# Eight matmuls on a constant tile at the start, and one single-use weight buffer instead of two

## The chip, the cores and the metric

The kernel runs on one core of a Trainium2 chip. The metric is the time of one execution in microseconds (us), here the median of several runs. TensorE is called PE in the profile, its weight load PEld, VectorE DVE, ScalarE ACT, GpSimd POOL, and SyncE, which issues most of the transfers, SP.

## The reference, cut to what matters

Two transformer blocks over 256 tokens of width 1024, all in float32. The first has three branches (spatial gating, convolution, pooling), a dense feed-forward and a gated embedding. The second has two kinds of attention and a mixture of 32 experts:

```python
def reference(x, ...):
    x = first_block(x, p, ...)       # rms_norm, w_in, three branches, w_out, feed-forward, embedding
    return second_block(x, c_2, ...) # attention, then experts, then a last rms_norm

def expert_block(args):              # for each of the 32 experts, on the tokens routed to it
    xb, e = args
    return (jax.nn.silu(xb @ w_gate[e]) * (xb @ w_up[e])) @ w_down[e]
```

The first step is `rms_norm(x, g_mix_pre)` and its product with `w_in`. The experts' weights are 3 x 1024 x 512 numbers for each expert, and all 32 are read whoever is routed to them.

## The kernel before, in words

Each engine has its own list of instructions, written by hand, and waits on semaphores. All weights pass once from HBM. There are two streams, both issued by SP in one fixed order.

The first stream, `load` (line 2338), brings the weights of everything but the experts, in pieces of 1 MB, into four buffers `raw`. For each piece ACT writes a rounded copy (`sph`, line 1180), POOL writes the remainder (`spl`, line 2310), and PE uses both in three matmuls (lines 492 to 494).

The second stream (line 2381) brings the experts' weights: `EXPERT_WEIGHTS` lists 192 pieces of 1 MB, four of gate and up weights (`in_gu`) for expert x and then two of down weights (`in_dn`) for expert x-1. Piece s goes into buffer `SLOT[place(s)]`. There are NS = 20 buffers that are used in turn: 18 halves of `ring0` to `ring8`, one at `ar(3072, 2048)`, and `slotx`. Two more are used once, at `ar(6144, 2048)` for piece 3 and `ar(8192, 2048)` for piece 4. Most buffers lie where something of the stages before lay, so each first use has a wait of its own in the loop that ends in line 2381. From piece 22 on, a piece waits until PE has used the piece that held its buffer before:

```python
                elif old:
                    kind0, x0, j0 = EXPERT_WEIGHTS[old[-1]]
                    if kind0 == "gu":
                        w.wait_ge(gu_mm, 4 * x0 + j0 + 1)
                    else:
                        w.wait_ge(down_mm, 2 * x0 + j0 + 1)
                e.dma_start(SLOT[i], I[kind][x, j]).then_inc(slot_sem[i], 16)
```

For each expert PE runs `gate_up` (line 1078), `turn` (lines 1093, 1099), `down` (line 1114) and `scatter` (line 1125), and for every fourth expert `gather` (line 1058). At the end come the last squares, roots and four stores.

The small tiles of the expert stage (`HN`, `SWT`, `HS`, `XG`, `YP`, `GFI`) lie in the same area `ar` as the single-use buffers.

At the start the work goes like this. SP loads `x` in two halves and then the first pieces. ACT squares each half (line 1220), takes the root (line 1194), DVE inverts it (line 1662), ACT makes a diagonal matrix of it (line 1199), and PE multiplies each block of `x` by the diagonal, which scales and transposes it (`norm_tile`, line 485; each such float32 matmul stands in the trace as two). Behind its two diagonals ACT has in its list the rounded copy of the first piece of weights (`split_one`), and only then the rounded copies of the normalized `x` (`high`, line 1208, tile `xah`). DVE writes the remainders (`low`, line 1677, tile `xal`), and PE's first product with weights waits for them. DVE's first instruction is the memset of a one-column tile `blank`, which ACT reads to load a table (`warm`, line 1170).

Of the kernel before, what the change touches and what calls it, by code (L numbers as in the profile page):

```python
# [20 lines left out]
NRAW = 4  # L21
# [79 lines left out]
def k8(t):  # L101
    return t.rearrange("p (k n) -> p k n", k=8)
# [105 lines left out]
def program(nc, I, out, const_at):  # L208
    with ExitStack() as ctx:
# [3 lines left out]
        ps = [ctx.enter_context(nc.psum_tensor(f"ps{i}", [128, 512], F32)) for i in range(8)]  # L213
        base = (nc.sbuf_base + 31) // 32 * 32

        def at(name, off, n, dt=F32, parts=128):

            assert base + 4 * (off + n) <= nc.sbuf_usable_end, (name, off, n)
            return nc.alloc_sbuf_tensor_at(name, [parts, n], dt, offset=base + 4 * off)[:, :]
# [29 lines left out]
        def ar(off, n, k=None):  # L249
            ar_n[0] += 1  # L250
            v = at(f"ar{ar_n[0]}", O_AR + off, n)
            return v if k is None else v.rearrange("p (k n) -> p k n", k=k)

        units, first, ada_at, ff_at, wide_at, conv_at = stream_plan()
# [2 lines left out]
        G = ar(0, 6144, 24)  # L257
        CV = ar(6144, 8 * 286, 8)
        CVO = ar(8432, 2048, 8)
        U = ar(10480, 2048, 8)  # L260
        V = ar(12528, 2048, 2)
        ZP = ar(12528, 8 * 272, 8)
# [40 lines left out]
        CWS = at("cws", O_XA + 1312, 36)  # L303

        SQA, SQ2 = ar(2048, 256), [ar(2304 + 256 * n, 256) for n in range(2)]
        HN = ar(1024, 2048, 2)
        w_out_units = [units[first["w_out_2"] + n] for n in range(4)]
        RING = ([at(f"ring{n}", TOP - 4096 - 4096 * n, 4096) for n in range(2)] +
                [at("ring2", O_RAW, 4096), at("ring3", O_XB, 4096), at("ring4", O_RAW + 4096, 4096)])
# [4 lines left out]
        SLOT = [r[:, 2048 * i:2048 * i + 2048] for r in RING for i in range(2)]  # L314
        SLOT.insert(8, ar(3072, 2048))
        SLOT.append(at("slotx", O_X, 2048))
        NS = len(SLOT)

        ONCE = {3: NS, 4: NS + 1}
        SLOT += [ar(6144, 2048), ar(8192, 2048)]  # L320

        def place(s):

            return ONCE.get(s, (s - (2 if s > 4 else 0)) % NS)

        RT = at("RT", 3040, 72).rearrange("p (t n) -> p t n", t=2)
        WC = at("WC", 3112, 64).rearrange("p (t n) -> p t n", t=2)
# [2 lines left out]
        FLAG = at("FLAG", 3368, 1, I32)  # L330
        SW = [ar(256 * n, 256) for n in range(2)]
        SE = [ar(512 + 256 * n, 256) for n in range(2)]
        SWT = [ar(6144 + 256 * n, 256) for n in range(2)]
        HS = [ar(6656 + 256 * n, 256) for n in range(2)]
        HE = [ar(10240 + 128 * n, 128) for n in range(2)]
        YP = [ar(8192 + 1024 * n, 1024) for n in range(2)]
        o_xg = (const_at["dist"][0] + 7) // 8 * 8
        XG = [k8(at("xg0", o_xg, 1024)), k8(ar(7168, 1024))]
        GFI = at("gfi", o_xg, 1024)
        JUNK, OUT = RING[4][:, 0:512], RING[5][:, 0:2048].rearrange("p (t n) -> p t n", t=2)  # L340


# [9 lines left out]
        def tap(k, c):  # L352
# [26 lines left out]
        slot_sem = [sem(f"d_slot{i}") for i in range(NS - NRAW)] + raw_sem  # L379
        d_x0, d_x1, d_idn, d_cst, d_col = (sem(n) for n in ("d_x0", "d_x1", "d_idn", "d_cst", "d_col"))  # L380
        d_ws, d_gmp, d_ada, d_gfp, d_p, d_wr, d_gfi, d_out = (sem(n) for n in (
            "d_ws", "d_gmp", "d_ada", "d_gfp", "d_p", "d_wr", "d_gfi", "d_out"))
        slot_sem += [d_gfp, d_wr]

        hi_ok, lo_ok, half_used = sem("hi_ok"), sem("lo_ok"), sem("half_used")

# [61 lines left out]

            return QK[kind][64 * (h % 2):64 * (h % 2) + 64, h // 2, :]

        slot_landed, per_slot = {}, [0] * (NS - NRAW) + [16 * sum(u.slot == i for u in units) for i in range(NRAW)] + [16, 16]
        for s, entry in enumerate(EXPERT_WEIGHTS):
            per_slot[place(s)] += 16
            slot_landed[entry] = per_slot[place(s)]
# [5 lines left out]
        def tensor(e):  # L460
            w = Seq(e)
# [112 lines left out]
            def channel_mean(name, src):  # L574

                b = bank(name)
                claim(b)
                e.matmul(ps[b][:, 0:256], mean, src, start=True, stop=True).then_inc(w.up(mean_mm), 1)
                return b


            cb = bank("conv")
# [67 lines left out]
            u = units[first["pool"]]  # L650
# [511 lines left out]
        def scalar(e):  # L1162
            w = Seq(e)
            begun = [0]

            def warm(func):

                w.wait_ge(blank_ok, 1)
                w.wait_ge(warm_ok, w.n(warm_ok))
                e.activation(warmed, blank, func).then_inc(w.up(warm_ok), 1)  # L1170

# [115 lines left out]
            for n in range(12):  # L1287
# [4 lines left out]
                if n == 8:  # L1292
                    w.wait_ge(cc_ok, 1)
                    w.wait_ge(mix_ok, 12)
                    e.activation(SQ, CVO, ACTF.Square).then_inc(w.up(sq_ok), 1)
            w.wait_ge(mean_mm, 2)
# [4 lines left out]
            def silu(c0):  # L1301

                w.wait_ge(cn_ok, 2)
                for c in (c0, c0 + 1):
                    e.activation(CVO[:, c, :], CVO[:, c, :], ACTF.Silu, bias=col("b_conv_ln", c),
                                 scale=col("g_conv_ln", c)).then_inc(w.up(silu_ok), 1)
# [16 lines left out]
            for n in range(4):  # L1323
                e.activation(XB[0][:, 2 * n:2 * n + 2, :], CVO[:, 2 * n:2 * n + 2, :], ACTF.Copy)\
                    .then_inc(w.up(act_hi), 1)
# [324 lines left out]
        def vector(e):  # L1650
            w = Seq(e)
# [45 lines left out]
            def conv(n, pairs=4):  # L1697

                for _ in range(n):
# [5 lines left out]
                    if k:  # L1705
                        w.wait_ge(tap_ok, w.n(tap_ok) - 1)
                        e.scalar_tensor_tensor(out=acc if k < 30 else CVO[:, c, :], in0=CV[:, c, k:k + 256],  # L1707
                                               scalar=tap(k, c), in1=acc, op0=ALU.mult, op1=ALU.add)\
# [5 lines left out]
                    tapped[:] = (pair, k, 1) if not i else (pair, k + 1, 0) if k < 30 else (pair + 1, 0, 0)  # L1714


            e.memset(blank, 1.0).then_inc(w.up(blank_ok), 1)
            w.wait_ge(d_idn, 16)
            for tt in range(2):
# [39 lines left out]
            def mix(i):  # L1759
# [10 lines left out]
                own()  # L1770
                e.tensor_tensor(k2(ps[b]), k2(ps[b]), U[:, 2 * i:2 * i + 2, :], ALU.mult).then_inc(w.up(mix_ok), 1)

# [13 lines left out]
            own()  # L1786
            e.tensor_reduce(TMP[:, 0:256], CVO.rearrange("p k n -> p n k"), AX, ALU.add).then_inc(w.up(cs_ok), 1)
            w.wait_ge(z_ok, 4)
# [530 lines left out]
        def sync(e):  # L2319
            w = Seq(e)  # L2320

            def load(a, b):

                for v in range(a, b):
                    u = units[v]
                    if v == first["qs1"]:
                        w.wait_ge(half_used, 2 * units[wide_at[10]].n + 2)
                        for i in range(2):
                            e.dma_start(SLOT[i], I["gu"][0, i]).then_inc(slot_sem[i], 16)
                    if v >= NRAW:  # L2330
                        old = units[v - NRAW]
                        if old.half:
                            w.wait_ge(lo_ok, 2 * old.n + 2)
                        elif v - NRAW in ada_at:
                            w.wait_ge(ada_ok, ada_used[ada_at.index(v - NRAW)])
                        else:
                            w.wait_ge(pool_mm, 4)
                    e.dma_start(RAW[u.slot], I["stream"][v]).then_inc(raw_sem[u.slot], 16)

            e.dma_start(X[:, 0, :], I["x"][0, 0:128, :]).then_inc(d_x0, 16)  # L2340
            e.dma_start(X[:, 1, :], I["x"][0, 128:256, :]).then_inc(d_x1, 16)
            load(0, NRAW)
            e.dma_start(CST[:, e0:cst_w], I["cst"][:, e0:cst_w]).then_inc(d_cst, 16)
            load(NRAW, len(units))

            def raws_free(*raws):

                for v in range(len(units) - NRAW, len(units)):
                    if units[v].slot in raws:
                        w.wait_ge(lo_ok, 2 * units[v].n + 2)  # L2350

            for s, (kind, x, j) in enumerate(EXPERT_WEIGHTS):
                i = place(s)
                old = [t for t in range(s) if place(t) == i]
                if s < 2:
                    continue
                if s == 2:
                    w.wait_ge(dt_mm, 8)
                elif s == 3:
                    w.wait_ge(dv_mm, 2)  # L2360
                elif s == 6:
                    raws_free(0, 1)
                elif s == 8:
                    w.wait_ge(half_used, 2 * units[first["vs"] + 1].n + 2)
                elif s == 10:
                    w.wait_ge(sv_mm, 2)
                elif s == 11:
                    raws_free(2)
                elif s == 12:
                    raws_free(3)  # L2370
                elif 13 <= s < 21:
                    w.wait_ge(half_used, 2 * w_out_units[min((s - 11) // 2, 3)].n + 2)
                elif s == 21:
                    w.wait_ge(y0_mm, 1)
                elif old:
                    kind0, x0, j0 = EXPERT_WEIGHTS[old[-1]]
# [6 lines that stand above are left out]
            for tt in range(2):  # L2383
                for nn in range(2):
                    c = slice(nn * 512, nn * 512 + 512)
                    w.wait_ge(*((fin_ok, 7 + tt) if nn else (so_ok, 7 + 3 * tt)))
                    e.dma_start(out[0, 128 * tt:128 * tt + 128, c], OUT[:, tt, c]).then_inc(d_out, 16)
# [177 lines left out]
```

## Time and profile before

| | |
|---|---|
| time, median of 3 runs | 1126.35 us (1125.43 to 1130.05) |
| the profiled execution, its own time | 1130.05 us |
| its span, first to last instruction | 1128.2 us |
| PE busy | 1029.6 us, 91% of the span |
| DVE, ACT, POOL busy | 507.7, 377.3, 494.0 us |
| moved by DMA | 342.16 MB, mean 303 GB/s |

All times of rows are counted from the span's start. The profiled execution is the slowest of the three. The 1.85 us between its time and its span lie outside of the instructions. A row of busy tenths has 40 slices of 28.2 us each.

### The profile page before, as it was taken

The numbers are of one execution on the slowest core, as the hardware profiler recorded it, in microseconds if no ns is written. First come the engines' busy times: TensorE is split into PE (matmuls) and PEld (weight loads), VectorE is DVE, ScalarE is ACT, GpSimd is POOL, SyncE is SP. The second block draws the span as 40 slices with busy tenths as digits, with TensorE's granted clock in tenths as the row PEclk, the third lists the DMA queues.
The fourth block names the chain that finished last, engine by engine and source line by source line (L and its number), as shares of the span: only waits on it lengthen the run. The fifth ranks groups of instructions, "written<-read, shape, count | busy, mean of one in ns | idle before, by whom it ended". The sixth has DMA issues, their size and how long they took to land.

```text
span 1128.2 us, 19730 instructions
## 1 busy us (share of the span) xinstructions
PE 1029.6 (91%) x8494; PEld 791.5 (70%) x8494; DVE 507.7 (45%) x904; ACT 377.3 (33%) x537; POOL 494.0 (44%) x209
## 2 busy tenths in 40 slices
PE   7999999999999999998999999899988778878677
PEld 6989999999799998887998895343443333424232
DVE  2998977565357666214345643322221221212113
ACT  7355544643663434446595332000000000000002
POOL 6886899867687777988565410000000000000000
PEclk9999999999999999999999999999999998989998
DMA  9554455456579888757333879999999999999995
GB/s 364 202 187 174 161 183 174 170 201 243 181 253 356 311 341 326 298 186 266 127 138 145 330 321 405 421 419 420 420 420 421 420 420 420 421 421 419 422 419 205
DMA packets 48330, 342.16 MB, mean 303 GB/s; under 512 B 5361, under 2 KB 5745, under 8 KB 7410
## 3 DMA queue, kind: packets, MB, share of 16 engines
q1 hardware_dynamic: 46944, 337.56, 75.6%
q10 hardware_dynamic: 1298, 3.32, 0.8%
q8 instruction: 68, 1.11, 0.4%
q14 instruction: 20, 0.16, 0.0%
HBM read 339.81 MB, written 1.05 MB: 302 GB/s over the span
## 4 chain that ended last, share of the span: by engine, by line
PE 60%; DMA 27%; DVE 5%; POOL 3%; ACT 3%; SPq 1%; issue 1%; DVEq 0%; ACTq 0%
DMA ring<-in_gu 19%; PE ps L492 14%; PE ps L494 14%; PE ps L493 14%; PE ps L1078 5%; DMA raw<-in_stream 4%; PE ps L1125 4%; POOL spl L2310 3%; DMA slotx<-in_dn 2%; PE ps L1114 2%; PE ps L1058 2%; SPq L2381 1%; PE ps L485 1%; ACT sph L1180 1%; DVE ps L1868 1%
## 5 line engine op out<-in xcount | busy, mean ns | idle before, releaser
L2310 POOL TENSOR_TENSOR spl<-raw,sph 128x1024 fp32r<-128x1024 f32 x204 | 493.6, 2451 | 162.3 <-ACT sph L1180 162.2
L1180 ACT ACTIVATE sph<-raw 128x1024 fp32r<-128x1024 f32 x204 | 205.8, 1053 | 144.6 <-DMA raw<-in_stream 91.9
L492 PE MATMUL ps<-xbh,sph 128*128 128x256 f32 x608 | 173.0, 285 | 5.8 <-DVE ps L1941 1.8
L493 PE MATMUL ps<-xbl,sph 128*128 128x256 f32 x608 | 172.0, 283 | 0.0
L494 PE MATMUL ps<-xbh,spl 128*128 128x256 f32 x608 | 172.0, 283 | 0.0
L492 PE MATMUL ps<-xah,sph 128*128 128x256 f32 x576 | 165.0, 286 | 1.1 <-DVE xal L1677 0.8
L493 PE MATMUL ps<-xal,sph 128*128 128x256 f32 x576 | 163.0, 283 | 0.0
L494 PE MATMUL ps<-xah,spl 128*128 128x256 f32 x576 | 162.9, 283 | 0.0
L2244 DVE TENSOR_TENSOR ar<-ar,ps 64x256 f32<-64x256 f32 x32 | 13.5, 423 | 266.5 <-ACT ar L1615 266.5
L1615 ACT ACTIVATE ar<-ps 64x256 f32<-64x256 f32 x32 | 12.1, 378 | 339.7 <-PE ps L1078 339.7
L1125 PE MATMUL ps<-ar,ar 128*128 128x512 f32 x256 | 123.9, 628 | 0.0
L492 PEld LDWEIGHTS ps<-xbh,sph 128*128 128x128 f32 x608 | 116.6, 192 | 7.4 <-DVE ps L1941 3.4
L494 PEld LDWEIGHTS ps<-xbh,spl 128*128 128x128 f32 x608 | 116.7, 192 | 0.0
L493 PEld LDWEIGHTS ps<-xbl,sph 128*128 128x128 f32 x608 | 116.6, 192 | 0.0
L492 PEld LDWEIGHTS ps<-xah,sph 128*128 128x128 f32 x576 | 110.5, 192 | 2.3 <-DVE xal L1677 0.9
L493 PEld LDWEIGHTS ps<-xal,sph 128*128 128x128 f32 x576 | 110.5, 192 | 0.4 <-issue 0.2
L494 PEld LDWEIGHTS ps<-xah,spl 128*128 128x128 f32 x576 | 110.5, 192 | 0.0
L1125 PEld LDWEIGHTS ps<-ar,ar 128*128 128x128 f32 x256 | 48.3, 199 | 64.7 <-issue 64.7
L1707 DVE SCALAR_TENSOR_TENSOR ps<-ar,COL,ps 128x256 f32<-128x256 f32 x232 | 92.1, 483 | 0.0
L1114 PE MATMUL ps<-ring,ar 128*32 128x512 f32 x456 | 56.9, 600 | 22.9 <-DVE ar L2252 13.8
L1078 PE MATMUL ps<-ring,ar 128*32 128x256 f32 x912 | 60.3, 395 | 17.9 <-DMA ring<-in_gu 17.8
L1078 PE MATMUL ps<-ring,xg 128*32 128x256 f32 x912 | 59.1, 397 | 11.7 <-DMA ring<-in_gu 11.7
(297 smaller groups left out, 1333.7 us busy)
## 6 DMA issues: line engine op xcount, KB each, us to landing
raw<-in_stream SPq DMA_DIRECT2D x127, 1024.0 KB, 5.1
ring<-in_gu SPq DMA_DIRECT2D x114, 1024.0 KB, 26.8
ring<-in_dn SPq DMA_DIRECT2D x57, 1024.0 KB, 27.1
ar<-in_gu SPq DMA_DIRECT2D x8, 1024.0 KB, 18.8
slotx<-in_gu SPq DMA_DIRECT2D x6, 1024.0 KB, 27.4
ar<-in_dn SPq DMA_DIRECT2D x4, 1024.0 KB, 27.7
slotx<-in_dn SPq DMA_DIRECT2D x3, 1024.0 KB, 26.3
X<-in_x SPq DMA_DIRECT2D x2, 512.0 KB, 4.7
```

Source lines behind the costliest of these rows:

```text
L492: e.matmul(o, sh, mh, start=start, stop=False)
L493: e.matmul(o, sh, ml, start=False, stop=False)
L494: return e.matmul(o, sl, mh, start=False, stop=stop)
L1058: mm = e.matmul(ps[b][:, (k - k0) * 128:(k - k0) * 128 + 128], HN[:, tt, k * 128:k * 128 + 128], SE[n][:, tt * 128:tt * 128 + 128], start= ...
L1078: mm = e.matmul(ps[b][32 * q:32 * q + 32, 0:256], XG[g % 2][:, k, (x % 4) * 32:(x % 4) * 32 + 32], W[:, q // 2, k % 2, (q % 2) * 256:(q % ...
L1114: mm = e.matmul(ps[bb[nn]][32 * j:32 * j + 32, :], HE[x % 2][:, 32 * j:32 * j + 32], W[:, 2 * (j % 2) + j // 2, :], start=True, stop=True)
L1125: mm = e.matmul(ps[yb[tt * 2 + nn]][:, :], SWT[x % 2][:, tt * 128:tt * 128 + 128], YP[x % 2][:, nn * 512:nn * 512 + 512], start=False, sto ...
L1180: e.activation(u.half(SPH[u.n % NSP], h), u.half(RAW[u.slot], h), ACTF.Copy).then_inc(w.up(hi_ok), 1)
L1615: e.activation(HS[x % 2][0:64, :], ps[bank_of["gu", x]][0:64, 0:256], ACTF.Silu)\
L1707: e.scalar_tensor_tensor(out=acc if k < 30 else CVO[:, c, :], in0=CV[:, c, k:k + 256], scalar=tap(k, c), in1=acc, op0=ALU.mult, op1=ALU.add)\
L2244: e.tensor_tensor(h[0:64, :], h[0:64, :], ps[bank_of["gu", x]][64:128, 0:256], ALU.mult)\
L2310: e.tensor_tensor(u.half(SPLO[u.n % NSP], h), u.half(RAW[u.slot], h), u.half(SPH[u.n % NSP], h), ALU.subtract).then_inc(w.up(lo_ok), 1)
```

## The change

It has two parts.

1. A tile `FILL` of 384 columns is set to 1.0 by DVE ahead of the memset of `blank`. PE waits for both memsets and then runs eight float32 matmuls of 128x128 by 128x256 on it, into bank 7, ahead of its first `norm_tile`. Nothing reads their result. ACT's `warm` waits for both memsets too.

2. Of the two single-use buffers the one at `ar(6144, 2048)` is gone. Piece 3 goes into buffer 3 of the ring, piece 4 into the single-use buffer at `ar(8192, 2048)`, and each later piece into the buffer after the one it had. The waits in SP's list are written for the piece numbers that now stand at the same buffers; piece 3 has no wait of its own, and piece 4 waits for the first `dv_mm` where piece 3 had waited for the second. `HN` moves to the area set free; `SWT`, `HS` and one `XG` move to where `HN` was, and the other `XG` to where the first `XG` was. `GFI` moves with its `XG`.

```diff
--- before.py
+++ after.py
@@ -257,6 +257,7 @@
         G = ar(0, 6144, 24)
         CV = ar(6144, 8 * 286, 8)
         CVO = ar(8432, 2048, 8)
+        FILL = ar(10480, 384)
         U = ar(10480, 2048, 8)
         V = ar(12528, 2048, 2)
         ZP = ar(12528, 8 * 272, 8)
@@ -303,7 +304,7 @@
         CWS = at("cws", O_XA + 1312, 36)
 
         SQA, SQ2 = ar(2048, 256), [ar(2304 + 256 * n, 256) for n in range(2)]
-        HN = ar(1024, 2048, 2)
+        HN = ar(6144, 2048, 2)
         w_out_units = [units[first["w_out_2"] + n] for n in range(4)]
         RING = ([at(f"ring{n}", TOP - 4096 - 4096 * n, 4096) for n in range(2)] +
                 [at("ring2", O_RAW, 4096), at("ring3", O_XB, 4096), at("ring4", O_RAW + 4096, 4096)])
@@ -316,12 +317,12 @@
         SLOT.append(at("slotx", O_X, 2048))
         NS = len(SLOT)
 
-        ONCE = {3: NS, 4: NS + 1}
-        SLOT += [ar(6144, 2048), ar(8192, 2048)]
+        ONCE = 4
+        SLOT.append(ar(8192, 2048))
 
         def place(s):
 
-            return ONCE.get(s, (s - (2 if s > 4 else 0)) % NS)
+            return NS if s == ONCE else (s - (s > ONCE)) % NS
 
         RT = at("RT", 3040, 72).rearrange("p (t n) -> p t n", t=2)
         WC = at("WC", 3112, 64).rearrange("p (t n) -> p t n", t=2)
@@ -330,13 +331,12 @@
         FLAG = at("FLAG", 3368, 1, I32)
         SW = [ar(256 * n, 256) for n in range(2)]
         SE = [ar(512 + 256 * n, 256) for n in range(2)]
-        SWT = [ar(6144 + 256 * n, 256) for n in range(2)]
-        HS = [ar(6656 + 256 * n, 256) for n in range(2)]
+        SWT = [ar(1024 + 256 * n, 256) for n in range(2)]
+        HS = [ar(1536 + 256 * n, 256) for n in range(2)]
         HE = [ar(10240 + 128 * n, 128) for n in range(2)]
         YP = [ar(8192 + 1024 * n, 1024) for n in range(2)]
-        o_xg = (const_at["dist"][0] + 7) // 8 * 8
-        XG = [k8(at("xg0", o_xg, 1024)), k8(ar(7168, 1024))]
-        GFI = at("gfi", o_xg, 1024)
+        XG = [k8(ar(2048, 1024)), k8(at("xg1", (const_at["dist"][0] + 7) // 8 * 8, 1024))]
+        GFI = ar(2048, 1024)
         JUNK, OUT = RING[4][:, 0:512], RING[5][:, 0:2048].rearrange("p (t n) -> p t n", t=2)
 
 
@@ -380,7 +380,7 @@
         d_x0, d_x1, d_idn, d_cst, d_col = (sem(n) for n in ("d_x0", "d_x1", "d_idn", "d_cst", "d_col"))
         d_ws, d_gmp, d_ada, d_gfp, d_p, d_wr, d_gfi, d_out = (sem(n) for n in (
             "d_ws", "d_gmp", "d_ada", "d_gfp", "d_p", "d_wr", "d_gfi", "d_out"))
-        slot_sem += [d_gfp, d_wr]
+        slot_sem.append(d_wr)
 
         hi_ok, lo_ok, half_used = sem("hi_ok"), sem("lo_ok"), sem("half_used")
 
@@ -448,7 +448,7 @@
 
             return QK[kind][64 * (h % 2):64 * (h % 2) + 64, h // 2, :]
 
-        slot_landed, per_slot = {}, [0] * (NS - NRAW) + [16 * sum(u.slot == i for u in units) for i in range(NRAW)] + [16, 16]
+        slot_landed, per_slot = {}, [0] * (NS - NRAW) + [16 * sum(u.slot == i for u in units) for i in range(NRAW)] + [16]
         for s, entry in enumerate(EXPERT_WEIGHTS):
             per_slot[place(s)] += 16
             slot_landed[entry] = per_slot[place(s)]
@@ -577,6 +577,11 @@
                 claim(b)
                 e.matmul(ps[b][:, 0:256], mean, src, start=True, stop=True).then_inc(w.up(mean_mm), 1)
                 return b
+
+
+            w.wait_ge(blank_ok, 2)
+            for _ in range(8):
+                e.matmul(ps[7][:, 0:256], FILL[:, 0:128], FILL[:, 128:384], start=True, stop=True)
 
 
             cb = bank("conv")
@@ -1165,7 +1170,7 @@
 
             def warm(func):
 
-                w.wait_ge(blank_ok, 1)
+                w.wait_ge(blank_ok, 2)
                 w.wait_ge(warm_ok, w.n(warm_ok))
                 e.activation(warmed, blank, func).then_inc(w.up(warm_ok), 1)
 
@@ -1714,6 +1719,7 @@
                     tapped[:] = (pair, k, 1) if not i else (pair, k + 1, 0) if k < 30 else (pair + 1, 0, 0)
 
 
+            e.memset(FILL, 1.0).then_inc(w.up(blank_ok), 1)
             e.memset(blank, 1.0).then_inc(w.up(blank_ok), 1)
             w.wait_ge(d_idn, 16)
             for tt in range(2):
@@ -2356,21 +2362,21 @@
                     continue
                 if s == 2:
                     w.wait_ge(dt_mm, 8)
-                elif s == 3:
-                    w.wait_ge(dv_mm, 2)
-                elif s == 6:
+                elif s == ONCE:
+                    w.wait_ge(dv_mm, 1)
+                elif s == 5:
                     raws_free(0, 1)
-                elif s == 8:
+                elif s == 7:
                     w.wait_ge(half_used, 2 * units[first["vs"] + 1].n + 2)
+                elif s == 9:
+                    w.wait_ge(sv_mm, 2)
                 elif s == 10:
-                    w.wait_ge(sv_mm, 2)
+                    raws_free(2)
                 elif s == 11:
-                    raws_free(2)
-                elif s == 12:
                     raws_free(3)
-                elif 13 <= s < 21:
-                    w.wait_ge(half_used, 2 * w_out_units[min((s - 11) // 2, 3)].n + 2)
-                elif s == 21:
+                elif 12 <= s < 20:
+                    w.wait_ge(half_used, 2 * w_out_units[min((s - 10) // 2, 3)].n + 2)
+                elif s == 20:
                     w.wait_ge(y0_mm, 1)
                 elif old:
                     kind0, x0, j0 = EXPERT_WEIGHTS[old[-1]]
```

## Rows read from the trace of the kernel before

**Rows 1.** The page: slices of the span, and the chain that ended last by line.
```profile
PE   7999999999999999998999999899988778878677
PEclk9999999999999999999999999999999998989998
DMA  9554455456579888757333879999999999999995
DMA ring<-in_gu 19%; PE ps L492 14%; PE ps L494 14%; PE ps L493 14%; PE ps L1078 5%; DMA raw<-in_stream 4%; PE ps L1125 4%; POOL spl L2310 3%; DMA slotx<-in_dn 2%; PE ps L1114 2%; PE ps L1058 2%; SPq L2381 1%; PE ps L485 1%; ACT sph L1180 1%; DVE ps L1868 1%
```

**Rows 2.** The chain that ended last, its start: start, duration, what.
```profile
0.75 4.04 DMA X<-in_x
7.10 4.36 PE ps L485 x20
11.55 1.57 ACT xah L1208 x4
```

**Rows 3.** The timeline of the start: start, duration, instruction, idle before and releaser.
```profile
0.82 0.06 DVE L1717 MEMSET SM<- 128x1 f32 x1 [0.82 <-PEq L2553]
1.66 1.28 ACT L1170 ACT_TABLE_LOAD   x1 [1.66 <-PEq L2553]
8.85 0.40 ACT L1199 ACTIVATE ar<-cst,SM 128x128 f32<-128x128 f32 x1 [0.23 <-DVE SM L1662]
9.15 1.99 ACT L1180 ACTIVATE sph<-raw 128x1024 fp32r<-128x1024 f32 x2
11.55 1.57 ACT L1208 ACTIVATE xah<-ps,COL 128x256 fp32r<-128x256 f32 x4 [0.41 <-PE ps L485]
12.42 4.33 DVE L1677 SCALAR_TENSOR_TENSOR xal<-ps,COL,xah 128x256 fp32r<-128x256 f32 x8 [3.61 <-ACT xah L1208]
```

**Rows 4.** Two windows of norm_tile: busy us and count of each engine, PEclk, DMA share, GB/s.
```profile
7.10:10.90 3.80, 3.80 (x18) 3.80 (x19) 0.17 (x1) 3.50 (x6) 0.63 (x1) 1.00 0.99 414
11.07:12.79 1.72, 1.72 (x16) 1.53 (x14) 0.37 (x1) 1.31 (x5) 1.72 (x2) 1.00 1.00 419
```

**Rows 5.** Other float32 rows: L659 in the chain, and the one wide memset of DVE.
```profile
227.09 6.91 PE ps L659 x32
L1884 DVE MEMSET ar<- 128x1024 f32 x1 | 0.9, 912 | 0.3 <-DVE pt L1687 0.3
```

**Rows 6.** What PE waited for between 16.5 and 300 us: total, times, longest.
```profile
PE ps L492 <- POOL spl L2310: 1.8, 3, 0.7
```

**Rows 7.** SP's issues of pieces 2 to 5, 12 to 13, 21, and 22 to 24.
```profile
617.57 0.33 SPq L2381 DMA_DIRECT2D ring<-in_gu  x1
622.97 1.52 SPq L2381 DMA_DIRECT2D ar<-in_gu  x2
624.53 0.43 SPq L2381 DMA_DIRECT2D ring<-in_gu  x1
...
656.57 0.81 SPq L2381 DMA_DIRECT2D ring<-in_gu  x2
...
675.96 0.33 SPq L2381 DMA_DIRECT2D slotx<-in_dn  x1
...
682.90 2.27 SPq L2381 DMA_DIRECT2D ring<-in_gu  x3
```

**Rows 8.** Windows of the expert stage, columns as in Rows 4.
```profile
683.00:685.00 2.00, 2.00 (x44) 1.17 (x37) 0.00 (x0) 0.38 (x2) 0.00 (x0) 1.00 0.59 160
695.00:1105.00 410.00, 342.48 (x3329) 156.13 (x3327) 93.21 (x204) 21.51 (x57) 0.00 (x0) 0.96 1.01 420
1100.00:1105.00 5.00, 4.61 (x22) 1.87 (x22) 0.00 (x0) 0.00 (x0) 0.00 (x0) 0.67 1.02 424
```

**Rows 9.** The chain that ended last: first DMA wait of the expert stage, and its end.
```profile
811.03 26.34 DMA slotx<-in_dn
...
1074.01 26.34 DMA ring<-in_gu
...
1100.39 1.94 PE ps L1078 x16
1102.33 4.12 PE ps L1125 x8
1106.45 1.91 PE ps L1078 x32
...
1112.43 3.63 PE ps L1125 x8
1116.06 1.85 PE ps L1114 x16
1117.91 0.05 issue
1117.96 1.11 PE ps L1125 x2
```

## The prediction, made before the changed kernel was run

> **What bounds the kernel now.** I read the slices of the page first [rows 1]. PE is busy nearly everywhere up to the 24th slice, and from the 25th on the DMA digit is 9 and PE's share falls. So there are two stages with different limits: up to about 680 us the time is made by PE and what feeds it, behind that by the experts' weights coming in. The chain by line says the same: the three matmul lines of the dense part hold 14% each, and `ring<-in_gu` alone 19% [rows 1]. Since the change touches the first 12 us and the buffers of the experts' stream, I then read those two places closely.
>
> At the start the chain goes x landing at 4.79, ACT, then PE's `norm_tile` from 7.10 for 20 rows and 4.36 us, then ACT's `xah` at 11.55 [rows 2]. The timeline adds what the chain hides: between its second diagonal (8.85) and `xah` ACT rounds the first weights, from 9.15 to 11.14, and only 0.41 us of idle stands between that and `xah` [rows 3]. Behind it DVE writes eight `xal` without a gap, 12.42 to 16.75, and PE's first product waits for them.
>
> The clock: the granted column reads 1.00 in both windows of `norm_tile`, but nothing is recorded that early, and the spacing of the rows tells more. 18 rows in 3.80 us are 211 ns each, 16 rows in 1.72 us are 108 ns each [rows 4]. The same instruction doubles its rate near 11.0 us, so it ran at 1.2 GHz before and at 2.4 GHz behind. PE had done nothing before 7.10; the clock rose 3.9 us after it began.
>
> In the expert stage the window 695 to 1105 has a DMA share of 1.01 and 420 GB/s [rows 8]. Nothing that PE does there can bring the weights faster. The last wait of the chain is a piece issued at 1074.01 that takes 26.34 us; from its landing at 1100.35 PE works to 1119.07 with hardly a wait [rows 9].
>
> **Part one, the filler.** DVE's only other wide memset takes 912 ns for 1024 columns [rows 5]; 384 columns are about 0.35 us. DVE starts at 0.82, so `blank` is ready near 1.3 instead of 0.9, and ACT's table load stands at 1.66 [rows 3]: hidden. If it were not, the next cover is the landing of x, two us behind the end of the table load.
>
> PE then starts near 1.4. Eight float32 matmuls are 16 rows of 256 columns. L659 has this shape and runs 32 rows in 6.91 us, 216 ns each at full clock [rows 5]; at half clock twice the 211 ns of 128 columns, 0.42 us. If the clock rises 3.9 us after the start, as it did behind 7.10, then nine rows run to 5.3 and seven take 1.5 us: the filler ends at 6.8, before `norm_tile` can begin. At half clock throughout it ends at 1.4 + 16 x 0.42 = 8.1.
>
> At full clock the first tile's 16 rows take 1.72 us from 7.10, the second waits for its diagonal at 9.25, and the 20th row, which releases `xah`, ends near 9.9 instead of 11.46. With the filler ending at 8.1 it is 8.1 + 20 x 0.108 + 0.2 = 10.5. Either way ACT is in `split_one` until 11.14 and is late next. So of 1.85 us that PE gains (18 rows x 0.103) only ACT's idle 0.41 us reaches `xah`. DVE's eight `xal` start from that, and PE's products from them. I take -0.4 us. The bounds are -1.9, if all of it counted, and +1.2, if the clock stayed low over filler and tiles (20 rows from 8.1 at 211 ns end at 12.6 against 11.46).
>
> The Trainium skill, "TensorE: Matmul & The Clock Gate", section "HAM oscillation — how this bites in real kernels", prices low clock at the throttled time times one half. By it 3.9 us are worth 2.0 us, and the sum below would end at +0.5 instead of +2.1. That rule prices PE's own time; it has no engine beside PE that is late anyway, as ACT is here.
>
> Does the 0.4 us reach the experts? PE's waits from 16.5 to 300 us come to 1.8 us in all [rows 6], and the rest of the way to 682 is chained by waits on one another, and between the first slice and the 25th the DMA digit is 9 once only [rows 1]. Nothing there is tied to a fixed time, so I let it pass whole.
>
> **Part two, the buffers.** No instruction is added on any engine; tiles only change their place, so `HN`, `SWT`, `HS`, `XG` and `GFI` cost nothing in themselves (a bank effect, if any, has no row; I take 0). What changes is how many pieces can be on chip before PE frees one. I counted the issues in SP's list. Before, four pieces (2 to 5) go out between 617.57 and 624.53 [rows 7]; then SP waits for the raw buffers. After, three pieces (2 to 4) fill the buffers that are free, and SP reaches the same wait with piece 5. From there each wait stands at the same buffer, so the same event sends a piece numbered one less: at 656.57 pieces 11 and 12 instead of 12 and 13, at 675.96 piece 20 instead of 21. When the first `gate_up` frees buffer 0 at 682.90, piece 21 goes out instead of 22. Piece 24 can go out a little earlier than 25 did, since buffer 3 now holds piece 3 and is free after PE's fourth step. From piece 25 on the predecessor is the piece 20 before, as it was.
>
> SP's own order: piece 3 no longer waits for `dv_mm`, and behind it only piece 4 was queued, which also goes earlier. That helps nothing, because all of it lands long before 682.
>
> So at 682.9 one piece more is still to come, and from then on DMA has no gap but 0.8 us just there: in 683 to 685 its share is 0.59 [rows 8], the same in both kernels. A piece is 1024 KB; at 420 GB/s that is 2.50 us. PE asks for pieces faster than they come, so the piece that ends the chain lands 2.50 us later. Bounds: 0 if the missing piece were made up in some gap (none is left after 685), and 3.3 if the gap of 0.8 came on top. I take +2.5, the value that the rows of the stage itself give.
>
> **Sum.** -0.4 + 2.5 = +2.1 us, with ends at -1.9 and +4.5. The profiled execution, 1130.05 us with a span of 1128.2, would be 1132.15 with a span of 1130.3. It lies 3.7 us above the median of the runs shown, so on the median, 1126.35, I forecast 1128.4 us, slower by 0.2%. A measurement of this kernel tells about 0.5% (5.6 us) from no change, so this is no change.
>
> **Rivals.** (a) The missing piece costs nothing: its place would be a gap in the stream after 685. For it: the chain meets no wait on DMA in this stage before 811 [rows 9]. Against it: the share of 1.01 over 410 us. Time: 1126.35 - 0.4 = 1125.9. (b) The clock's gain passes whole, -1.9, if ACT's wait on PE counted more than the profile shows; 1126.35 - 1.9 + 2.5 = 1126.9. Against it stands ACT busy until 11.14. (c) The filler does not raise the clock or comes too late: +1.2 + 2.5, 1130.1. For it: I know only one rise, and it came after 3.9 us. (d) Slower beyond 0.5%: the tail runs at half clock. From 1100.39 to 1119.07 PE's rows on the chain are 1.94, 4.12, 1.91, 3.63, 1.85, 1.11 and smaller ones, some 17 us [rows 9], and PE comes to them from waiting for weights. In 1100 to 1105 the granted clock was 0.67 [rows 8], so about 3.3 us were at 1.2 GHz, and a scatter took 4.12 instead of 3.63. A stretch of low clock costs half its length; with +2.1 given, 3.5 us more are needed, that is 7 us more at half clock. With an earlier starved PE this could happen in many executions: 1132 or more.
>
> On (d) the Trainium skill, the same page, section "Loop structure matters more than you think", says that a long wait for a transfer between matmuls drops the clock and the next ones run at half rate. It speaks against this change; the trace agrees in kind (0.96 over the stage [rows 8]) and not in size.
>
> **How the numbers follow.** My forecast 0.60, (a) 0.16, (b) 0.10, (c) 0.07, (d) 0.04, and 0.03 for something faster beyond 0.5% that no row shows. The forecast's own range is 1127 to 1130. Taking in the bounds of the sum (1124.5 to 1130.9) and that executions of one kernel lie up to 3.7 us above their median, the range is 1124.6 to 1131.4. Within 0.5%: 0.60 + 0.16 + 0.10 + 0.07 = 0.93; slower 0.04; faster 0.03.
>
> **What the profile of the changed kernel would show.** 16 rows of the filler from about 1.4 us; `norm_tile` at 108 ns a row; `xah` at about 11.15 with no idle on PE's account; PE's first product 0.4 us earlier; the first issue behind the raw wait unchanged but for that shift, `slotx` again near 675.5, buffer 0 near 682.5; DMA share 1.01 to the end, and a last gate piece that lands at 1102.4 instead of 1100.35. Wrong would be: `xah` well before 11.1 (then something else stood in ACT's list), a last landing at or before 1100.3, or a tail of more than 19 us from that landing to the end of PE's rows.

## The result, and the profile after

The changed kernel takes 1133.17 us (median of 4 runs, 1132.1 to 1134.09) beside 1126.36 us (4 runs, 1125.43 to 1130.05). The ratio is 1.0051 with a 95% interval of 1.003 to 1.0074, that is 5.7 us more (3.4 to 8.3). I had forecast 1128.4 and a range up to 1131.4. The record has nine more executions of the changed kernel; the median of all thirteen is 1132.15 us (1129.79 to 1137.22), 1.0 less than that of the four.

The profiled execution of after took 1130.97 us, 0.92 more than that of before, where I had forecast 2.1 more. It is a fast one of its kernel (the third of thirteen), while that of before is the slowest of its four, so their difference can't be read as that of the kernels. What each stage took can be compared. First the head of the page of after:

```profile
span 1128.9 us, 19763 instructions
PE   8999999999999999998999998989978888888676
PEclk9999999999999999999999999999998999989899
DMA  9555455456479898756344689999999999999994
PE 57%; DMA 27%; POOL 5%; DVE 4%; ACT 3%; SPq 2%; issue 1%; DVEq 0%; ACTq 0%
```

The shape is that of [rows 1]: PE nearly everywhere until the 24th slice, DMA at 9 behind it. Now the start, from the timeline of after (start, length, what, idle before and its releaser):

```profile
0.90 0.38 DVE L1722 MEMSET ar<- 128x384 f32 x1 [0.90 <-PEq L2559]
1.35 5.50 PE L584 MATMUL ps<-ar 128*128 128x256 f32 x16 [1.35 <-DVE SM L1723]
1.66 1.28 ACT L1175 ACT_TABLE_LOAD   x1 [1.66 <-PEq L2559]
5.05 1.06 ACT L1225 ACTIVATE ar<-X 128x1024 f32<-128x1024 f32 x1 [1.90 <-DMA X<-in_x]
7.34 4.25 PE L485 MATMUL ps<-ar,X 128*128 128x128 f32 x32 [0.48 <-ACT ar L1204]
9.39 1.99 ACT L1185 ACTIVATE sph<-raw 128x1024 fp32r<-128x1024 f32 x2
11.28 0.45 ACT L1213 ACTIVATE xah<-ps,COL 128x256 fp32r<-128x256 f32 x1
12.14 4.33 DVE L1682 SCALAR_TENSOR_TENSOR xal<-ps,COL,xah 128x256 fp32r<-128x256 f32 x8 [3.09 <-ACT xah L1213]
```

The filler runs from 1.35 to 6.85 and the table load stays at 1.66, as forecast. Behind the filler `norm_tile` needs 1.86 us for its first 16 rows, 116 ns each where the first rows took 211 in [rows 4], so it runs at 2.4 GHz from its start. `xah` no longer waits for PE (no idle in its row, 0.41 us in [rows 3]): it follows `sph`. x landed 0.23 us later here, so the starts don't show the gain. The time from ACT's first square of x to `xah` does: 6.73 us before (4.82 to 11.55), 6.23 here.

The windows of after (length, busy time and rows of PE, PEld, DVE, ACT and POOL, granted clock, DMA share, GB/s), which answer to [rows 8]:

```profile
683.00:685.00 2.00, 2.00 (x46) 1.14 (x38) 0.13 (x1) 0.38 (x1) 0.00 (x0) 1.00 1.00 373
695.00:1105.00 410.00, 342.78 (x3310) 154.20 (x3309) 91.00 (x198) 19.99 (x53) 0.00 (x0) 0.95 1.01 420
1100.00:1105.00 5.00, 5.00 (x42) 2.12 (x40) 0.00 (x0) 0.00 (x0) 0.00 (x0) 1.00 1.01 419
```

The weights come at the same 420 GB/s. The first line doesn't answer to that of [rows 8], since the stage began 4.5 us earlier here; at the same place in the stage, 678.5 to 680.5, the DMA share is 0.60 (0.59 before), so the short gap is there in both. SP's list, from the timeline of after, shows the pieces that [rows 7] showed before:

```profile
613.09 0.80 SPq L2387 DMA_DIRECT2D ring<-in_gu  x2
615.88 0.33 SPq L2387 DMA_DIRECT2D ar<-in_gu  x1
630.66 2.02 SPq L2387 DMA_DIRECT2D ring<-in_gu  x3
671.46 0.33 SPq L2387 DMA_DIRECT2D slotx<-in_dn  x1
678.41 0.33 SPq L2387 DMA_DIRECT2D ring<-in_dn  x1
```

Three pieces (2 to 4) go out, and then SP waits. The first piece that waits for `gate_up` is now a down piece, number 21, where it was a gate piece, number 22. So one piece more is still to come.

The end of the chain, which answers to [rows 9]:

```profile
1080.51 27.74 DMA ar<-in_dn
1108.25 0.04 issue
1108.30 1.06 PE ps L1119 x8
...
1110.20 3.63 PE ps L1130 x8
1113.83 1.85 PE ps L1119 x16
1115.69 0.05 issue
1115.73 1.11 PE ps L1130 x2
```

All of PE's rows here are at full clock. The chain now hangs on piece 189, a down piece. The forecast had named the gate piece 185, which the chain hung on before, and 1102.4 for its landing; it landed at 1098.35, which by the forecast's own list is a sign of being wrong. It is none, since the stage began 4.5 us earlier: counted from the first expert matmul it landed 2.49 us later than before, as forecast. From 1108.25 to the end of PE's rows it is 8.6 us. What I had not read lies behind the last store. SP's waits in 1123 to 1130, first before, then after (in all, times, longest):

```profile
SPq L2389 <- PEq L2389: 0.2, 1, 0.2
SPq L2398 <- PEq L2398: 0.2, 1, 0.2
```

```profile
SPq L2404 <- PEq L2404: 3.2, 1, 3.2
SPq L2395 <- PEq L2395: 0.2, 1, 0.2
```

SP's last wait on PE has grown from 0.2 to 3.2 us. Between the two waits stands a branch: `with nc.If(flag > 0)` in `general`, which jumps over the code for a case that doesn't occur with this input. Every engine takes it. Its instructions, in the listing of that line (min/median/max ns, first and last start), before and after:

```profile
L2399 ACTq COMPARE_BRANCH  x1: 50/50/50, 1127.0 to 1127.0; - x1
L2399 PEldq COMPARE_BRANCH  x1: 369/369/369, 1127.1 to 1127.1; - x1
L2399 SPq COMPARE_BRANCH  x1: 50/50/50, 1127.6 to 1127.6; - x1
```

```profile
L2405 ACTq COMPARE_BRANCH  x1: 50/50/50, 1124.8 to 1124.8; - x1
L2405 PEldq COMPARE_BRANCH  x1: 3729/3729/3729, 1124.9 to 1124.9; - x1
L2405 SPq COMPARE_BRANCH  x1: 50/50/50, 1125.4 to 1125.4; - x1
```

The same branch takes 0.37 us on PE before and 3.73 us after, and the same 0.05 to 0.07 us as before on the other engines. From the first store's issue to the span's end it is 4.85 us before (1123.35 to 1128.2) and 7.82 after (1121.12 to 1128.94), 2.97 us more. That is a little less than the 3.36 us on PE: before, PE was through at 1127.45 and SP came to its own branch only at 1127.6, so part of PE's time lay behind SP's.

The spans come out of their stages as follows; the last landing is that of piece 191.

| us | before | after |
|---|---|---|
| to the first expert matmul | 681.77 | 677.28 |
| from there to the last landing | 433.41 | 435.90 |
| from there to the first store's issue | 8.17 | 7.95 |
| from there to the end | 4.85 | 7.82 |
| span | 1128.20 | 1128.94 |

The second line is the buffer, +2.49. The fourth is the branch, +2.97. The first hides most of both in this pair: 4.5 us less, of which the filler can have given 0.5 and the rest is a spread between executions (last section).

### The profile page after: what moved, and what is told of

Same layout as the page of the kernel before. It is cut to its first block, busy times and chain, and to the rows that moved or that the text cites. A ratio compares the mean times of both kernels' runs of the same rounds, so it can differ in the third digit from the quotient of the medians.

```text
span 1128.9 us, 19763 instructions
## 1 busy us (share of the span) xinstructions
PE 1033.6 (92%) x8510; PEld 792.3 (70%) x8510; DVE 508.8 (45%) x905; ACT 376.9 (33%) x537; POOL 494.0 (44%) x209
## 4 chain that ended last, share of the span: by engine, by line
PE 57%; DMA 27%; POOL 5%; DVE 4%; ACT 3%; SPq 2%; issue 1%; DVEq 0%; ACTq 0%
DMA ring<-in_gu 15%; PE ps L492 13%; PE ps L494 13%; PE ps L493 13%; PE ps L1083 5%; POOL spl L2316 5%; DMA raw<-in_stream 5%; PE ps L1130 4%; DMA ar<-in_gu 3%; DMA ar<-in_dn 2%; DMA ring<-in_dn 2%; PE ps L1119 2%; PE ps L1063 2%; SPq L2387 2%; ACT sph L1185 1%
## 5 line engine op out<-in xcount | busy, mean ns | idle before, releaser
L1083 PE MATMUL ps<-ring,xg 128*32 128x256 f32 x928 | 62.4, 402 | 18.0 <-DMA ring<-in_gu 17.8
L1083 PEld LDWEIGHTS ps<-ring,xg 128*32 128x32 f32 x928 | 28.3, 113 | 58.6 <-issue 31.4
```

The lines of the kernel that those rows point to most:

```text
L1083: mm = e.matmul(ps[b][32 * q:32 * q + 32, 0:256], XG[g % 2][:, k, (x % 4) * 32:(x % 4) * 32 + 32], W[:, q // 2, k % 2, (q % 2) * 256:(q % ...
```

## The experiments

In all of them the branch's duration on PE and the stage times are read from one profile each, the medians from several runs. The median of before was 1126.47 us beside the first four kernels (32 runs), 1127.5 beside the next four (18 runs) and 1126.98 beside the last three (21 runs).

My theory: three terms add up, the filler's -0.4, the buffer's +2.5, and +3.0 from PE's branch, whose place in the program the filler's 32 PE instructions (16 matmul rows and 16 weight loads) have moved. (The expectations below count the whole 3.4 us of PE's branch; 3.0 of them reach the end.) The rivals: the filler costs time in some other way (its work, its tile, the clock); the longer branch comes from the smaller number of buffers; the buffer's price is not a piece.

**One part each.** The first kernel is before with the filler alone, the second before with one single-use buffer alone.

```diff
+            w.wait_ge(blank_ok, 2)
+            for _ in range(8):
+                e.matmul(ps[7][:, 0:256], FILL[:, 0:128], FILL[:, 128:384], start=True, stop=True)
... (cut: the tile FILL and the second memset that `warm` waits for, as in the change)
+            e.memset(FILL, 1.0).then_inc(w.up(blank_ok), 1)
```

> Part one alone: the kernel before with the filler of eight matmuls, both single-use buffers kept. Theory J (the filler's 32 PE instructions move the branch behind the expert stage, so that its target has to be fetched): PE's branch at the very end lasts about 3.7 us instead of 0.37, and the kernel is 3.4 - 0.4 = 3.0 us slower than before. Rival W (the forecast's own working: the filler only helps): branch 0.4 us, kernel 0.4 us faster. Rival B (all of the loss comes with the buffer): no slower than before.

Measured: 1131.05 us (1128.37 to 1133.59, 9 runs), ratio 1.0038 (1.0023 to 1.0053), that is +4.3 us (2.6 to 6.0). The branch took 3869 ns.

```diff
-        ONCE = {3: NS, 4: NS + 1}
-        SLOT += [ar(6144, 2048), ar(8192, 2048)]
+        ONCE = 4
+        SLOT.append(ar(8192, 2048))
... (cut: the waits and the moved tiles, as in the change)
```

> Part two alone: one single-use buffer, no filler. The forecast's term: 2.5 us slower than before, branch at the end 0.37 us as before, DMA share 1.01 from 695 on, and at the time when the first buffer of the ring is freed the piece issued is number 21. Rival B: 6 to 7 us slower, all that was measured. Rival J2 (the buffer costs nothing, everything is the branch): within 0.5 us of before.

Measured: 1130.01 us (1126.6 to 1133.58, 12 runs), ratio 1.0029 (1.0015 to 1.0043), +3.3 us (1.7 to 4.8). The branch took 475 ns, and from the first expert matmul to the last landing it was 435.96 us. So the branch belongs to the filler, and the piece to the buffer.

**The branch's place without the filler's work.** Before, with 64 waits on a semaphore that has long been reached, at the start of PE's list. They compile to 32 instructions, as many as the filler has.

```diff
+            for _ in range(64):
+                e.wait_ge(blank_ok, 1)
             cb = bank("conv")
```

> The kernel before with 64 waits on a semaphore that is already up ahead of PE's first matmul, which compile to 32 instructions: as many as the filler has, no work for TensorE and no warmer clock; PE is idle there until 7.1 us and 32 of them need some 2 us. Theory J: branch at the end 3.7 us, kernel 3.4 us slower than before. Rival (the filler's matmuls themselves cost the time, by clock or by contention): no change, branch 0.37 us.

Measured: 1129.82 us (1126.96 to 1133.08, 12 runs), ratio 1.0015 (0.9996 to 1.0034), +1.7 us (-0.5 to 3.8). The interval holds 0, 3.0 and the 3.4 of the expectation, so the times decide nothing; the profile does. The listing of the branch's line:

```profile
L2401 ACTq COMPARE_BRANCH  x1: 50/50/50, 1124.8 to 1124.8; - x1
L2401 PEldq COMPARE_BRANCH  x1: 3839/3839/3839, 1124.8 to 1124.8; - x1
```

With no filler and with both buffers the branch is long. So what the instructions ahead of it do is not what counts.

**The filler with half the instructions.** After, with four matmuls of 512 columns instead of eight of 256: the same columns, 16 instructions.

```diff
-        FILL = ar(10480, 384)
+        FILL = ar(10480, 640)
...
-            for _ in range(8):
-                e.matmul(ps[7][:, 0:256], FILL[:, 0:128], FILL[:, 128:384], start=True, stop=True)
+            for _ in range(4):
+                e.matmul(ps[7][:, 0:512], FILL[:, 0:128], FILL[:, 128:640], start=True, stop=True)
```

> The changed kernel with the filler as four matmuls of 512 columns: the same work for PE in 16 instructions instead of 32. Theory J: the branch stands 16 instructions earlier; if its target is then in what PE has fetched, the branch lasts 0.37 us and the kernel is 2.5 - 0.4 = 2.1 us slower than before, as forecast; if not, 3.7 us and 5.5 us slower. Rival (the loss grows with the filler's work, not with its instructions): as the changed kernel, 6.8 us slower, with a short branch.

Measured: 1129.72 us (1128.18 to 1132.0, 12 runs), ratio 1.0029 (1.0016 to 1.0041), +3.3 us (1.8 to 4.6):

```profile
L2405 PEldq COMPARE_BRANCH  x1: 475/475/475, 1125.0 to 1125.0; - x1
```

The branch is short again, and from the first expert matmul to the last landing it is 436.5 us, 3.1 more than before. Beside the kernel with one buffer and no filler (+3.3 us, on the same chip) this one shows the filler with a short branch: the two measured the same, so no cost or gain of it shows there.

**The version that the terms point to.** Both single-use buffers and the filler of four matmuls.

> The kernel before with both single-use buffers and the filler as four matmuls of 512 columns (16 PE instructions, few enough to keep the branch short). Forecast of both causes together (branch 3.4, buffer 2.5, filler -0.4): branch 0.4 to 0.5 us, from PE's first expert matmul to the last landing 433.4 us as before, and 0.4 us faster than before, which is within the scatter of the runs. If the filler costs something by itself that the branch does not explain: 1 to 2 us slower.

Measured: 1128.57 us (1125.42 to 1132.98, 12 runs) beside 1127.5, ratio 1.0012 (0.9997 to 1.0027). The branch took 378 ns, and the stage to the last landing 433.7 us. The expected -0.4 us lies just outside of the interval (-0.3 to 3.0 us). The same kernel once more, on another chip:

> Filler as four matmuls of 512 columns, both single-use buffers, once more, since its first interval (-0.3 to +3.0 us) left open whether the filler helps or costs. Filler's gain: 0.4 us faster than before. Filler costs something: 1 us slower or more.

1128.01 us (1126.09 to 1134.71, 11 runs) beside 1126.98, ratio 1.0012 (0.9995 to 1.0028). Neither measurement shows a gain.

**More places of the branch.** Before with 256 and with 128 instructions more, as 16 or 8 waits ahead of each `gate_up`, one execution each.

```diff
                 if x < NE:
+                    for _ in range(16):
+                        e.wait_ge(blank_ok, 1)
+                if x < NE:
                     gate_up(x, (0, 1))
```

> The kernel before with 16 more waits on a semaphore that is up ahead of each expert's first gate_up, which compile to 8 PE instructions each, 256 in all: one whole block of PE's program as its fetches are seen in the trace (16 KB each, 64 bytes an instruction). If what counts is where the branch stands within a block: 0.4 us, like before. If more PE instructions in general lengthen it: 3.7 us or more.

> The same with 8 waits ahead of each expert, 128 instructions in all: half a block. If the place within a block counts, the target is in a block not yet fetched: 3.7 us, although there are fewer instructions than in the kernel with 256. If only the number counts, it would lie with the longer one.

Measured, the branch's line with 256 more (one execution of 1125.26 us) and with 128 more (1129.67 us):

```profile
L2402 PEldq COMPARE_BRANCH  x1: 375/375/375, 1122.3 to 1122.3; - x1
```

```profile
L2402 PEldq COMPARE_BRANCH  x1: 3772/3772/3772, 1123.7 to 1123.7; - x1
```

256 instructions more leave the branch short, 128 make it long. It is not their number in itself but where the branch comes to lie in a pattern that 256 instructions leave as it was.

**No single-use buffer.** Before with 20 buffers only, no filler.

> Part two doubled: no single-use buffer at all, no filler. The buffer's theory: another 2.5 us, 5.0 us slower than before; from PE's first expert matmul to the last landing 433.4 + 5.0 = 438.4 us; branch 0.4 us. Rival (only the first lost buffer counts, since the gap in the stream moves): 2.5 us, 435.9 us.

Measured: 1131.88 us (1129.87 to 1138.03, 7 runs), ratio 1.0047 (1.0028 to 1.0066), +5.3 us (3.2 to 7.4). First expert matmul to last landing: 438.2 us. Two buffers 433.4, one 435.9, none 438.2: a piece each.

**Sixteen instructions, no filler.** The 64 waits cut to 32.

> Control for it: the kernel before with 32 waits at PE's start, 16 instructions, no filler. Branch 0.4 us; the same as before. Against the kernel with the filler it shows the filler alone at the same place of the branch: 0.4 us slower than that one by the forecast.

Measured: 1127.43 us (1125.83 to 1133.08, 11 runs), ratio 1.0007 (0.9992 to 1.0023). The branch took 475 ns.

**After with a short branch.** After with 14 waits ahead of each `gate_up`, 224 instructions, so that the filler's 32 and they are 256.

> The changed kernel whole (eight filler matmuls, one single-use buffer) with 7 more PE instructions ahead of each expert, 224 in all, so that with the filler's 32 the branch stands one whole block (256) later than in the kernel before. If the place of the branch is what the forecast missed: branch 0.4 to 0.5 us instead of 3.7, and 2.1 us slower than before, as forecast for the change, instead of the 5.7 to 6.8 that the change showed. If the filler or the moved tiles cost something else: slower by 5 us or more with a short branch.

Measured: 1130.52 us (1129.9 to 1132.67, 5 runs), ratio 1.0043 (1.0028 to 1.0058), +4.9 us (3.2 to 6.5):

```profile
L2408 PEldq COMPARE_BRANCH  x1: 369/369/369, 1126.8 to 1126.8; - x1
```

The branch is short once more, though the filler is all there. But the expected 2.1 us are missed: the time is 2.8 us above the -0.4 + 2.5 of the other two terms, and the interval shuts them out. Of this, 0.8 us shows in the profile: 436.7 us to the last landing instead of 435.9. The added waits stand in that stage, but the 4x512 kernel took 436.5 there without them. The rest is open. Against after itself, which was measured apart from it, this kernel is 2.7 us faster by the median of the four executions and 1.6 by that of the thirteen, where the branch should give 3.0.

All kernels by the branch:

| instructions more on PE | kernels | branch on PE, ns | first store's issue to the end, us |
|---|---|---|---|
| 0 | before, one buffer, no buffer | 369 to 475 | 4.8 to 4.9 |
| 16 | 4x512 filler (two kernels, one of them twice), 32 waits | 378 to 475 | 4.8 to 4.9 |
| 32 | after, filler alone, 64 waits | 3729 to 3869 | 7.8 to 8.0 |
| 128 | waits | 3772 | 7.9 |
| 256 | waits, after with waits | 375, 369 | 4.8 to 4.9 |

## Why the forecast missed

**The step that failed** is the costing of part one by what its instructions do at the start. The prediction counts 16 rows of the filler in PE time and opens part two with "No instruction is added on any engine"; nowhere does it ask what 32 more PE instructions do to the rest of the program. They move the branch at the end. The missing term is +3.0 us. It read the end only up to the PE row that ends at 1119.07; the 4.85 us between the first store's issue and the end, where the branch of before stands with its 0.37 us, were taken as fixed without being read.

What the branch waits for is shown in part. The DMA view of after has one more transfer of instructions in the window 1124 to 1130 than that of before, here before and then after (packets, MB, share):

```profile
q8 instruction: 1, 0.02, 1.3%
```

```profile
q8 instruction: 2, 0.03, 2.5%
```

The added one starts at 1125.9, 1.0 us after PE's branch began, and carries 16 KB; the other one starts in both kernels 0.7 us after the branch has ended. Ahead of the branch this queue had made 67 transfers for 17201 recorded instructions of PE, which is 64 bytes for each and 256 in a transfer. In the compiled program of before the branch is PE's instruction 17209, in after 17241, and its target is some 380 further on. With 0, 16, 32 and 128 instructions more, 67 transfers had been made when PE came to the branch, with 256 more it was 68: so the target moved on while what PE had brought in did not, until a whole block was added.

The Trainium skill, "Runtime: NRT & Kernel Launch", section "Instruction fetch mechanics", says that instructions come in sequential 16 KiB blocks, and that a taken branch whose target has not been brought in must wait for a transfer. The case agrees with that in kind; no run here shows how large PE's store of instructions is. Between 16 more (short) and 32 more (long) lies a border that I did not locate. Counted from the program's first instruction, a multiple of 256 passes the target only at some 69 more, so why the border lies there is not shown.

**The filler at the start** was right in mechanism, and a little too large. It ended at 6.85 (forecast 6.8), `norm_tile` ran at 2.4 GHz, and ACT's `split_one` was late next. From the first square of x to `xah` it is 6.28 to 7.02 us in the seven profiles without filler (mean 6.63) and 6.23 to 6.48 in the six with it (mean 6.38): 0.25 us on the mean, for a term of 0.4. The term came from ACT's idle of 0.41 us in one profile [rows 3], and that idle varies: without filler `xah` waited for PE by 0.70 us in one profile, and in others not at all, as `sph` was the later one. In the kernel without single-use buffers and with 128 instructions of waits:

```profile
11.87 1.21 ACT L1203 ACTIVATE xah<-ps,COL 128x256 fp32r<-128x256 f32 x3 [0.70 <-PE ps L480]
```

```profile
11.32 1.57 ACT L1211 ACTIVATE xah<-ps,COL 128x256 fp32r<-128x256 f32 x4
```

What the filler gives is at most this wait.

**That this gain reaches the end** was assumed and is not borne out. The two measurements of the 4x512 filler beside both buffers gave +1.4 us each (-0.3 to 3.0, and -0.6 to 3.2), where -0.4 was expected. The filler alone stands 1.7 us above its sum of -0.4 + 3.0, after with a short branch 2.8 above its own. Against that, the 32 waits alone gave +0.8 (-0.9 to 2.6), so that only 0.6 us lie between them and the filler on the same chip, and beside one buffer the kernels with the 4x512 filler and without measured the same. The dense stage shows no such loss: from the first product to the first expert matmul it was 663.8 to 669.0 us with filler (mean 665.4) and 663.6 to 668.2 without (mean 665.0). In the expert stage, up to the last landing, there may be one: with both buffers it is 433.7 to 434.5 us in three profiles with filler and 433.3 to 433.9 in five without; with one buffer 435.9, 436.5 and 436.7 with, 436.0 without. Why, these runs don't show. Whether the filler costs about one microsecond, or nothing, stays open.

**The buffer** was right in mechanism and size: +2.5 forecast, 2.49 between the two profiles and 2.5 between the kernel with one buffer and the five with both and no filler (435.96 against 433.5 on the mean). The piece numbers moved by one as counted, and the DMA share stayed at 1.01.

**The rivals.** (a) The missing piece costs nothing: wrong, by the three steps of 433.4, 435.9 and 438.2. (b) The clock's gain passes whole: wrong, 0.25 of 1.85 us, and never more than the 0.7 that `xah` waited. (c) The filler is too late: wrong, it ended 0.5 us before `norm_tile`. (d) A tail at half clock: not in the profiled execution of after, whose window 1100 to 1105 was granted 1.00 (0.67 in [rows 8]). The slower ones have no trace; the slowest, 1137.22 us, also had the lowest mean clock of the thirteen, 0.970 against 0.974 to 0.983, so there it may have had a part. PE's lag does occur in kernels with both buffers: with 64 and with 32 waits PE's last rows ended 8.1 and 7.9 us behind the last landing, against 6.2 in after. In the window 1095 to 1105 of the kernel with 32 waits:

```profile
1095.00:1105.00 10.00, 8.74 (x48) 3.64 (x52) 0.00 (x0) 0.00 (x0) 0.00 (x0) 0.66 0.97 406
```

The granted clock was 0.66 on the mean there, so a part of it was at 1.2 GHz, and PE still had work left when the last weights were there. From the last landing to the first store's issue it was 9.8 and 9.6 us in these two, 7.9 to 8.5 in all the others, so such a lag costs up to 1.9 us; it was not what slowed the profiled execution of after.

**The sum and the range.** With the measured terms it is -0.25 + 2.5 + 3.0 = +5.25 us, inside of the measured 3.4 to 8.3. With the branch in it my sum would have been -0.4 + 2.5 + 3.0 = +5.1 and the forecast 1131.45, just past the end of my range. The measured median is 1.7 us above that, the median of all thirteen executions 0.7. The range itself was not worked out as it says: its bound of 1130.9 with the 3.7 us of scatter on top is 1134.6, not 1131.4. That would have held the result, but by width and not by mechanism. The filler's upper bound was also a little too high: 20 rows of 211 ns from 8.1 end at 12.3, not at 12.6.

## What to carry to other kernels

Look at what the end of a program does after its last store, and whether a branch stands there: here instructions added at the program's start, or before each expert, made it 3.4 us longer, and a full 256 of them left it short. Before work is put down to an edit's own cost, run the same number of empty instructions in its place. In a stage that is all DMA, as here, a buffer less ahead of it costs one piece at the stage's rate when no later gap gives it back.

## What the runs showed of the hardware that I had not expected

**A branch over code that isn't run costs PE 0.37 to 0.48 us or 3.73 to 3.87 us**, and nothing between, in thirteen profiles. Which of the two it was went with the number of PE instructions ahead, whatever they did. The other engines took it in 0.05 to 0.07 us in every kernel.

**The dense stage has a spread of its own.** It took 663.6 to 666.3 us in eleven of thirteen profiles, and 668.2 in that of before and 669.0 in one of the 4x512 filler with both buffers. The transfers of `raw` are slower in those two. The windows 400 to 450 of before and after:

```profile
400.00:450.00 50.00, 45.65 (x366) 44.60 (x366) 33.32 (x45) 20.43 (x25) 36.61 (x17) 1.00 0.84 323
```

```profile
400.00:450.00 50.00, 49.37 (x387) 48.11 (x387) 38.20 (x48) 21.38 (x27) 40.00 (x18) 1.00 0.89 345
```

Before moved 323 GB/s and PE was busy for 45.65 us, after 345 and 49.37. A transfer of 1 MB took 7.3 us there from issue to landing (median), 7.5 in the other late profile, and 6.7 to 7.0 in the other eleven. The same kernel took 669.0 us in one execution and 666.3 in another, on another chip, so it is not the code; whether it is the execution or the chip is not shown. This is most of the 4.5 us by which after led at the first expert matmul, and it hid most of the change in the pair of profiles.
